# A prefetch hint for the jump back, on three engines of the expert loop of a two-layer trunk

## The reference

```python
D_MODEL = 1024; SEQ = 256; N_EXPERTS = 8; TOP_K = 2; D_FF_EXPERT = 3584

def swiglu(h, w_gate, w_up, w_down):
    return (jax.nn.silu(h @ w_gate) * (h @ w_up)) @ w_down

def moe_swiglu(h, w_router, w_gate, w_up, w_down):
    logits = (h @ w_router).astype(jnp.float32)
    top_val, top_idx = lax.top_k(logits, TOP_K)
    top_w = jax.nn.softmax(top_val, axis=-1)
    gates = jnp.sum(jax.nn.one_hot(top_idx, N_EXPERTS, dtype=jnp.float32) * top_w[..., None], axis=-2)
    out = jnp.zeros_like(h)
    for e in range(N_EXPERTS):
        out = out + gates[..., e:e + 1] * swiglu(h, w_gate[e], w_up[e], w_down[e])
    return out

def reference(x, ...):
    for i in range(DEPTH):
        ...  # norm, mixer, norm, add
        h = rms_norm(x, norm_g[i, 2])
        if i % 2 == 0:
            y = swiglu(h, ffn_w_gate[slot], ffn_w_up[slot], ffn_w_down[slot])
        else:
            y = moe_swiglu(h, moe_w_router[slot], moe_w_gate[slot], moe_w_up[slot], moe_w_down[slot])
        x = x + rms_norm(y, norm_g[i, 3])
    return x
```

## Time and profile before

| | us |
|---|---|
| median of 3 runs | 1273.4 |
| lowest and highest of them | 1270.49, 1274.1 |
| the profiled execution, its time | 1276.08 |
| its span | 1274.2 |
| start of the four turns' code on TensorE after the jump: turns 2, 3, 4 | 612.4, 833.8, 1055.7 |
| TensorE busy | 1221.2 (96% of the span) |
| mean granted TensorE clock | 0.985 |

### The profile page before, as it was taken

How to read it: one execution, slowest core, us unless ns; L and a number is a source line. 1 busy time by engine, 2 the same in 40 slices (tenths; PEclk the granted TensorE clock), 3 DMA queues, 4 the chain that set the end, 5 groups by cost and what they waited for, 6 DMA issues and landing times.

```text
span 1274.2 us, 16146 instructions
## 1 busy us (share of the span) xinstructions
PE 1221.2 (96%) x6044; PEld 854.6 (67%) x6044; DVE 689.5 (54%) x783; ACT 539.2 (42%) x522; POOL 106.9 (8%) x118
## 2 busy tenths in 40 slices
PE   9999999989989999998899999889999988999996
PEld 7888887778877888334688833568883346888332
DVE  3844445656578888102688710268861026886102
ACT  2643444455445776002577500257750025775001
POOL 0000000000003050100005010000501000050100
PEclk8999999999999999999999999999999999999998
DMA  9755553853266999999999999999999999999995
GB/s 314 257 187 178 196 178 120 199 188 131 100 248 225 372 363 360 347 409 414 413 415 406 368 371 408 415 414 415 407 346 386 407 415 414 415 406 341 391 407 209
DMA packets 141294, 412.58 MB, mean 324 GB/s; under 512 B 9683, under 2 KB 29139, under 8 KB 141142
## 3 DMA queue, kind: packets, MB, share of 16 engines
q1 hardware_dynamic: 140406, 408.23, 84.5%
q0 software_dynamic: 816, 3.28, 0.8%
HBM read 410.44 MB, written 1.05 MB: 323 GB/s over the span
## 4 chain that ended last, share of the span: by engine, by line
PE 85%; DMA 5%; DVE 3%; SPq 3%; issue 3%; ACT 1%; DVEq 0%; ACTq 0%
PE bank L1395 19%; PE bank L1396 19%; PE bank L1397 19%; PE bank L1768 13%; DMA raw<-in_moe_w_gate 4%; PE bank L1781 4%; SPq L545 3%; PE bank L1721 1%; PE bank L1402 1%; PE bank L1844 1%; PE bank L1491 1%; PE bank L1798 1%; PE bank L1657 1%; DMA head_row<-in_heads 1%; ACT w_hi L604 1%
## 5 line engine op out<-in xcount | busy, mean ns | idle before, releaser
L906 DVE TENSOR_TENSOR raw_lo<-raw,w_hi 128x2048 fp32r<-128x2048 f32 x149 | 339.8, 2300 | 101.4 <-ACT w_hi L604 101.2
L604 ACT ACTIVATE w_hi<-raw 128x2048 fp32r<-128x2048 f32 x149 | 284.5, 1916 | 148.3 <-PE bank L1397 95.7
L1395 PE MATMUL bank<-w_hi,h_hi 128*128 128x512 f32 x568 | 230.2, 405 | 19.4 <-DVE h_lo L1249 9.8
L1396 PE MATMUL bank<-raw_lo,h_hi 128*128 128x512 f32 x576 | 229.9, 399 | 9.1 <-issue 9.1
L1397 PE MATMUL bank<-w_hi,h_lo 128*128 128x512 f32 x568 | 226.5, 399 | 0.0
L1395 PEld LDWEIGHTS bank<-w_hi,h_hi 128*128 128x128 f32 x568 | 109.6, 193 | 50.2 <-DVE raw_lo L906 17.2
L1768 PE MATMUL bank<-raw,h_b 128*64 128x512 f32 (+1 forms) x768 | 143.1, 524 | 0.0
L1396 PEld LDWEIGHTS bank<-raw_lo,h_hi 128*128 128x128 f32 x576 | 111.1, 193 | 33.1 <-issue 10.4
L1397 PEld LDWEIGHTS bank<-w_hi,h_lo 128*128 128x128 f32 x568 | 109.2, 192 | 23.9
L906 DVE TENSOR_TENSOR raw_extra_lo<-raw_extra,w_hi 128x2048 fp32r<-128x2048 f32 x48 | 111.4, 2348 | 15.4 <-ACT w_hi L604 15.4
L1768 PEld LDWEIGHTS bank<-raw,h_b 128*64 128x64 f32 x768 | 53.7, 137 | 82.6 <-issue 74.5
(11 more groups left out here) (311 smaller groups left out, 1601.9 us busy)
## 6 DMA issues: line engine op xcount, KB each, us to landing
raw<-in_moe_w_gate SPq DMA_DIRECT2D x96, 1024.0 KB, 11.4
raw<-in_moe_w_up SPq DMA_DIRECT2D x80, 1024.0 KB, 11.8
raw<-in_moe_w_down SPq DMA_DIRECT2D x64, 1024.0 KB, 12.6
raw_extra<-in_moe_w_down SPq DMA_DIRECT2D x48, 1024.0 KB, 13.9
raw_extra<-in_moe_w_up SPq DMA_DIRECT2D x32, 1024.0 KB, 12.7
raw_extra<-in_moe_w_gate SPq DMA_DIRECT2D x16, 1024.0 KB, 7.4
raw<-in_ffn_w_gate SPq DMA_DIRECT2D x11, 1024.0 KB, 5.1
raw<-in_ffn_w_up SPq DMA_DIRECT2D x11, 1024.0 KB, 5.1
```

The costliest lines, as they stand in the source:

```text
L604: nc.scalar.activation(to, raw_slot(source), ACT.Copy).then_inc(hi_ready, 1)
L906: nc.vector.tensor_tensor(lo_slot(source), raw_slot(source), high.bitcast(f32), ALU.subtract).then_inc(lo_ready, 1)
L1395: mm(out, a_hi, b_hi, start=first, stop=False)
L1396: mm(out, a_hi, b_lo, start=False, stop=False)
```

## The change

```diff
@@ scalar @@
-            with sc.Fori(0, pairs) as p:
+            with nc.Fori(0, pairs, engines=[sc.engine], hint_back_edge=True) as p:
@@ vector @@
-            with ve.Fori(0, pairs) as p:
+            with nc.Fori(0, pairs, engines=[ve.engine], hint_back_edge=True) as p:
@@ tensor @@
-            with pe.Fori(0, pairs) as p:
+            with nc.Fori(0, pairs, engines=[pe.engine], hint_back_edge=True) as p:
```

## The result

| | before | after |
|---|---|---|
| median of the runs, us | 1272.72 | 1259.33 |
| lowest and highest | 1270.49, 1274.1 | 1257.13, 1263.21 |
| the profiled execution, its time | 1276.08 | 1263.21 |
| its span | 1274.2 | 1261.0 |
| the first turn's last wait for `h_lo` to the end of the span | 673.2 | 656.8 |

The ratio is 0.99, with a 95% interval from 0.9871 to 0.9929: 13.4 us faster (four runs of each kernel). A second set, six runs of after and eleven of before, gave 1259.71 beside 1276.01 us, ratio 0.9869 (0.9828 to 0.9911), 16.3 us faster. The forecast was 1257.0 us with 16.4 us of gain, in a range from 1253 to 1270.

A forecast was written before the change was run, and what follows sets the result against it. TensorE was taken as the bound, with code-fetch stalls at three seams. Stalls 3.9 us plus clock 1.6 us made 5.5 us per seam, 16.4 us in all, from 1273.4 to 1257.0 us; range 1253 to 1270.

The forecast's parts named there:

- The bound and where the gain lies: TensorE, busy 1221.2 of 1274.2 us, bounds the kernel; the gain lies in its code-fetch waits at the three seams.
- First stall: TensorE's wait at the jump back for the target block's code goes: 2.1 us per seam.
- Second stall: TensorE's wait after ten matmuls for the next code block shrinks to 1.4 us; 3.9 us earlier, first stall included.
- Clock: The 1.2 GHz stretch behind TensorE's second stall goes, as its idle gets shorter: 1.6 us per seam, ends 0 and 1.6.
- The sum: Both stalls and the clock give 5.5 us per seam, 16.4 us over three seams, ends 8 and 17.4.
- The room in the lull: The loads' slack late in each turn, 6.8 us of idle, has room for the 5.5 us won at the seam.
- Only the first stall goes: Rival at TensorE's seam: the second block is still asked for late; 2.1 us per seam, 1267.0 us, chance 0.14.
- The hint does nothing: Rival at TensorE's jump: the hint, given at the top of the turn, fetches nothing; 1273.4 us, chance 0.13.
- The hint takes the place of the sequential prefetch: Rival: from hint to jump every code block is fetched only when needed; slower, 1375 to 1430 us, chance 0.05.
- The loads take it back: Rival: the lull is no slack, loads keep 221 us a turn; 0 to 3 us per seam, middle 1269, chance 0.05.
- VectorE and ScalarE, nothing: Their loop bodies largely stay in their engines, so their hints win nothing; at worst one fetch of some 3 us per turn.

The follow-up runs named there:

- the kernel with no slow clock: After, with the head of TensorE's loop moved to the first slot of a code block, first run: 1259.77 us, ratio 0.9891.
- the added matmuls: Unused matmuls before TensorE's jump back: 16 on before, 1283.99 us; 8 and 32 on after with its head at the block's start, 1269.98 and 1279.59 us.

## Why the prediction was right, step by step

**The bound and where the gain lies.** Right. The two stalls were code fetches, they lay only at the seams, and the gain is in TensorE alone.

**First stall, 2.1 us a seam.** Right, at all three seams, and the packet moves ahead of the jump as forecast. It moves at 608.0 and not near 605 because the seam itself comes 3.2 us later in this profile: behind the wait for `h_lo`, the forecast is 4.0 us and the packet 3.8.

**Second stall, forecast as 1.4 us of idle.** Right in mechanism, and in size as a mean (2.20, 0.65 and 0.34 are 1.06). I took the time from the engine's entry into the target block to the first matmul of the second as 5.47 us, and put the entry at 608.5, which is 7.5 us behind the matmul that follows the wait for `h_lo` (601.01). The hint's record gives the entry: 6.4, 6.4 and 6.2 us behind that matmul. From there to the second block's first matmul it is 5.7, 5.8 and 5.7 us. So the entry is 1.1 to 1.3 us earlier than I took it, the time is 0.2 to 0.3 longer, and the second block starts 12.1, 12.2 and 11.9 us behind the wait, not 13.0. The step that I had wrong is what sets the entry: not the front end's pace alone, but the target's own packet, which moves 3.6 to 3.9 us behind the wait and can be used 2.5 to 2.6 us later. Until then the branch waits. Before, at the time of that packet, the one for the block behind the jump moved; this is the eleventh packet of the earlier trace rows, gone in after.

That also says why the three stalls differ. The second block comes at the same time behind the wait in all three. In the first seam there is no slow clock behind the wait, so TensorE gets through its matmuls 1.6 us sooner, and it stands those 1.6 us longer.

**Clock, 1.6 us a seam.** The sum was right, the stretch was partly another. Before, each seam had two slow stretches and not one: the one of the earlier trace rows behind the second stall, and one behind the wait for `h_lo`. The second of these can be read from the earlier trace rows beside the timeline of after: from that matmul to L1887 it is 608.27 - 601.01 = 7.26 us before and 609.89 - 604.22 = 5.67 after, the same work, 1.6 us apart. After has one slow stretch a seam. In the second and third seam it is the one behind `h_lo` (827.49 - 820.18 = 7.31), and the one behind the second stall is gone, as forecast. In the first seam it is the other way round, against the forecast. The window behind the 2.20 us stall reads:

```profile
616.60:619.90 3.30, 3.30 (x9) 2.62 (x8) 1.62 (x2) 1.91 (x1) 0.00 (x0) 0.50 1.03 411
```

I had reasoned that 2.14 us of idle had cost no clock and that a shorter one would not either. The 2.20 us here did, and so did 2.11 us in the first seam of the kernel with its head at the block's start and no hint, while 3.25 us did not in the one with the hint. The length of one idle alone doesn't decide it. The profiled execution lost one stretch of two in every seam, and so did the second profile of after, there always the one behind `h_lo` being left (in its third seam it lasts 13 matmuls, elsewhere 7). The kernel without a hint had two in its first seam and none in the others.

**The sum and its arrival.** From the first seam's wait to the end of the span it was 673.2 us and is 656.8: 16.4 us, the sum of the forecast to the tenth, as 5.5 + 6.7 + 4.2 us. That agreement to the tenth is luck: the clock's part varies, and the median gained 13.4 us, 3.0 less than forecast, in the second set 16.3. The profiled execution shows 13.2 us in its span because the loop started late. Its first matmul in after and in before:

```profile
405.46 0.50 PE L1395 MATMUL bank<-w_hi,h_hi 128*128 128x512 f32 x1 [2.39 <-DVE raw_lo L906]
```

```profile
400.27 0.79 PE L1395 MATMUL bank<-w_hi,h_hi 128*128 128x512 f32 x1 [2.31 <-DVE raw_lo L906]
```

The 5.2 us (of which the first turn made up 2.0) lie ahead of the loop and so of the first jump back. Slow clock in the stages there is what the trace shows for them. One window of after, and the same of before (another such stretch lies from 377 to 382 us, at 0.66):

```profile
261.00:270.00 9.00, 6.87 (x38) 6.90 (x39) 0.00 (x0) 1.52 (x1) 0.00 (x0) 0.62 0.61 227
```

```profile
261.00:270.00 9.00, 7.75 (x60) 7.08 (x61) 2.33 (x2) 2.42 (x3) 0.00 (x0) 1.00 0.65 228
```

Over the profiled executions of this case the loop starts between 397.2 and 405.7 us, with and without hints (405.44 with VectorE's and ScalarE's alone, 400.28 for the same kernel a second time). This spread is why one profile can't be compared with another by its span, and why the medians differ from the forecast by 2 us and say 13.4 or 16.3 us of gain in two sets of runs.

**The room in the lull, 6.8 us a turn.** Right, and it is the term that turned out to matter most. 221.4 and 221.9 us could come down to 214.7 at best, 6.7 to 7.2 us, and no kernel went below. That the loads make this floor was argued from the earlier trace rows. For it speak the waits for `w_down` that TensorE has in the kernel with no slow clock, the pace of 410 to 412 GB/s in the turns at the floor (88.5 MB at 411 GB/s are 215.3 us), and the added matmuls, which come through only in part. One reading of the prediction was wrong, without harm to the sum: that the loads set the pace from the lull to the next seam. In that part of a turn of before TensorE waits 3.3 us for `h_lo` and 0.5 us for `w_down`, and is busy otherwise. ScalarE's long wait costs nothing there: its high part is done at 595.94 + 1.91 = 597.85 us, and TensorE starts at 601.01, held by `h_lo`. A run that changes the loads themselves was not made.

**The rivals.** Only the first stall goes: the medians exclude it (1267.0), and the second stall shrank. The hint does nothing: excluded. The Trainium skill's rule (Runtime: NRT & Kernel Launch, Instruction fetch mechanics) that prefetch is purely sequential holds in this case only for loops without a hint: with it, the target's packet lies 3.8 us ahead of the first matmul that needs it, and the measurement decides. The number of lines that the prediction cites from the Trainium skill (Advanced Engine Details and Errata, ISA Cache), two, stands there beside "32KB (128KB on TensorE)", which would be eight lines. No run here tells the two apart, since a body of 2111 instructions is longer than eight lines as well. The hint takes the place of the sequential prefetch: excluded for all blocks but one, and there the packets show just this, to good effect, because the block that it displaces is never used. The loads take it back: not at the size of this change, but it is what stopped the next one, the head at the block's start.

**VectorE and ScalarE, nothing.** Right, by two runs.

## What to carry to other kernels

When a "wait for nothing" comes as often as a loop jumps back, look at the code queue and at the length of the branch's own record. In this kernel the two waits were code fetches. Where the target's packet comes late, a hint on the back edge moved it ahead, though not when the jump lay 15 instructions into its block. Where a second stall comes a few instructions behind the jump, the place of the loop's head in its block was the cause, and moving the head cured it without a hint. Before counting such a gain, look for the resource that is next: here the loads leave 6.8 us a turn, the hint uses 5.5 to 6.7, and after that even a perfect seam gives next to nothing.

## What the runs showed of the hardware

- The hint is not acted on where it stands. With 41 and 63 instructions between the start of the last block and the jump, the target's packet moves where the packet of the block behind the jump would have moved, and the stall is gone. With 15 it moves 3.5 to 3.7 us after the branch begins, as without a hint, and the stall is back in full (2.3 us).
- The next block in sequence is fetched when the engine enters a block: its packet moves 3.1 to 3.3 us after the first instruction of the target block, and its first matmul runs about 2.5 us after the packet.
- A jump to a block that isn't there holds TensorE's sequencer for 5.9 to 6.2 us, and the array for 2.0 to 2.3 us of it in this kernel (3.3 us where less work was queued). When the block was there in time, the jump took 0.4 us. When the head lies 22 instructions ahead of a block's end it costs 2.8 to 3.1 us more.
- An idle of 3.25 us was in one kernel followed by full clock, and one of 2.11 us in another by 3.3 us at 1.2 GHz, which cost 1.6 us. The first seam of after had no slow clock behind its wait for `h_lo` in one profile, and half the clock there in the other.
